# Two weight sums of a seven-product block: adding DMAs inside SBUF in place of VectorE additions

## The reference

```
h = rmsnorm(x, norm_mix);  proj = h @ w_in                    # 2048 -> 3*1024 + 4
q, k, v: 4 heads of 256;   cum = cumsum(log_sigmoid(gate logits))
p = softmax(q k^T / 16 + cum_t - cum_s, keys s <= t)
x = x + merge_heads(p v) @ w_out
h = rmsnorm(x, norm_ffn)
x = x + (silu(h @ w_gate) * (h @ w_up)) @ w_down              # 2048 -> 5632 -> 2048
out = rmsnorm(x, final_norm)
```

## Time and profile before

| What | Value |
|---|---|
| median of 3 runs | 1839.42 us (1839.38 to 1840.31) |
| the profiled execution's own time | 1841.1 us |
| its span, first to last instruction | 1839.3 us |
| mean granted TensorE clock | 0.993 |
| PE, DVE, ACT, POOL busy | 98%, 61%, 36%, 3% of the span |

### The profile page before, as it was taken

One profiled execution on the slowest core, in us unless ns is written; L12 is line 12 of the kernel. 1 busy time (PEld: TensorE's weight loads), 2 busy tenths in 40 slices (PEclk: granted clock), 3 DMA queues, 4 the chain that ended last, 5 costly groups with the idle time before them and its releaser, 6 DMA issues.

```text
span 1839.3 us, 29804 instructions
## 1 busy us (share of the span) xinstructions
PE 1807.1 (98%) x11560; PEld 1647.4 (90%) x11560; DVE 1115.5 (61%) x1277; ACT 659.0 (36%) x867; POOL 58.5 (3%) x82
## 2 busy tenths in 40 slices
PE   8999999999799999999999999999999999999998
PEld 6888888888698999989989999899899899998996
DVE  5332432337875766757757667577477575674774
ACT  5232232334342433424424324234243243342444
POOL 3000000004000000000000000000000000000005
PEclk9999999999899999999999999999999999999999
DMA  7323322332133432343333333323333333234332
GB/s 229 87 75 92 91 68 91 143 132 69 46 93 100 115 118 82 93 127 94 102 93 101 112 109 93 117 81 120 98 92 104 104 115 108 77 110 119 92 138 92
DMA packets 268389, 189.55 MB, mean 103 GB/s; under 512 B 7280, under 2 KB 236656, under 8 KB 267376
## 3 DMA queue, kind: packets, MB, share of 16 engines
q1 hardware_dynamic: 265872, 181.46, 33.7%
q10 hardware_dynamic: 2400, 6.29, 0.9%
HBM read 183.54 MB, written 4.19 MB: 102 GB/s over the span
## 4 chain that ended last, share of the span: by engine, by line
PE 92%; DVE 4%; ACT 2%; issue 1%; POOL 1%; DMA 0%; ACTq 0%; POOLq 0%; DVEq 0%
PE ps L1423 45%; PE ps L1635 31%; PE ps L1642 15%; DVE tmp L1027 1%; DVE hT_lo L1015 1%; DVE qq L1338 1%; POOL xres L656 0%; DVE sy L1338 0%; PE ps L1436 0%; DVE oT_lo L1343 0%; ACT split_hi L853 0%; DMA xres<-in_x_dram 0%; DVE split_lo L1217 0%; DVE split_lo L1008 0%; PE ps L1478 0%
## 5 line engine op out<-in xcount | busy, mean ns | idle before, releaser
L853 ACT ACTIVATE split_hi<-raw 128x1024 fp32r<-128x1024 f32 x378 | 399.9, 1058 | 781.8 <-DVE raw L1231 387.7
L1217 DVE TENSOR_TENSOR split_lo<-raw,split_hi 128x1024 fp32r<-128x1024 f32 x378 | 462.0, 1223 | 331.5 <-ACT split_hi L853 331.5
L1423 PE MATMUL ps<-split_hi,hT_hi 128*128 128x512 f32 x704 | 274.2, 389 | 1.0 <-DVE hT_lo L1259 1.0
L1423 PE MATMUL ps<-split_lo,hT_hi 128*128 128x512 f32 x704 | 274.0, 389 | 0.0
L1423 PE MATMUL ps<-split_hi,hT_lo 128*128 128x512 f32 x704 | 273.9, 389 | 0.0
L1635 PE MATMUL ps<-hT_hi,split_hi 128*128 128x256 f32 x1008 | 247.8, 284 | 0.0
L1635 PE MATMUL ps<-hT_lo,split_hi 128*128 128x256 f32 x1008 | 247.3, 283 | 0.0
L1231 DVE TENSOR_TENSOR raw<-raw 128x1024 f32<-128x1024 f32 x168 | 205.2, 1221 | 9.6
L1635 PEld LDWEIGHTS ps<-hT_hi,split_hi 128*128 128x128 f32 x1008 | 193.4, 192 | 2.2 <-issue 2.0
L1635 PEld LDWEIGHTS ps<-hT_lo,split_hi 128*128 128x128 f32 x1008 | 193.4, 192 | 0.1
L1423 PE MATMUL ps<-hT_hi,split_hi 128*128 128x512 f32 (+1 forms) x464 | 171.2, 369 | 0.8 <-DVE split_lo L1008 0.8
(11 more groups left out here) (173 smaller groups left out, 2594.3 us busy)
## 6 DMA issues: line engine op xcount, KB each, us to landing
raw<-in_ffn_w_gate_up_dram SPq DMA_DIRECT2D x172, 512.0 KB, 4.2
raw<-in_ffn_w_down_dram SPq DMA_DIRECT2D x80, 512.0 KB, 4.1
raw<-in_fox_w_in_dram SPq DMA_DIRECT2D x24, 1024.0 KB, 5.7
raw<-in_fox_w_out_dram SPq DMA_DIRECT2D x8, 1024.0 KB, 5.1
xres<-in_x_dram SPq DMA_DIRECT2D x4, 1024.0 KB, 8.2
xres<-in_x_dram ACTq DMA_DIRECT2D x4, 1024.0 KB, 8.5
raw<-in_ffn_w_down_dram SPq DMA_DIRECT2D x4, 1024.0 KB, 5.6
out_dram<-xres SPq DMA_DIRECT2D x16, 256.0 KB, 3.1
```

Source lines behind the costliest of these rows:

```text
L853: nc.scalar.activation(ring(0, n), source, ACT.Copy).then_inc(t_hi, 1)
L1217: nc.vector.tensor_tensor(ring(1, n), source, f32(ring(0, n)), ALU.subtract).then_inc(t_lo, 1)
L1423: ins = nc.tensor.matmul(bank, stationary(sp, t), moving(mp, t), start=first and t == tiles[0] and (sp, mp) == PASSES[0], stop=last and t ...
```

## The change

The third sum (B12 + B22) and the fourth (B11 + B21) are no longer made by VectorE. GpSimd issues a DMA for each, from SBUF to SBUF, which adds B22 to what lies in B12's slot, and B21 to what lies in B11's slot. `t_sum` now counts two sums per unit, and two new semaphores, `sum_in`, are raised when an adding DMA has landed; ScalarE waits for these before parts 4 and 6. Before each DMA GpSimd adds a 128 by 1 tile to itself (`turn_of`) and raises `turns`, on which the next one waits. GpSimd waits for the second sum before the first DMA, and for the low half of part 2 and B21's load before the second. SP's waits on the third and fourth sum become waits on the low halves of parts 4 and 6. ScalarE waits for the low half of part n-2 before it copies part n.

```diff
     def sums(self, j):
-        return counted(8, 16, self.r, 4 * self.nth + j)
+        return counted(4, 8, self.r, 2 * self.nth + j)
+    def summed(self):
+        return 16 * (self.nth + 1) if self.r is None else 64 * self.r + 16 * (2 + self.nth + 1)
...
# SP, load_units; the same two edits in load_group, and the second one ahead of load_last(1)
-                    sp.wait_ge(t_sum, at.sums(3))
+                    sp.wait_ge(t_lo, at.part(4))
                     load_part(r, "B22", u + 1)
...
-                    sp.wait_ge(t_sum, at.sums(4))
+                    sp.wait_ge(t_lo, at.part(6))
                     load_part(r, "B21", u + 1)
...
# GpSimd, between its work for the second norm and for the last
+            def add_part(at, j, into, other):
+                x1, x2 = (slot(place(at.r, name, at.u)[0]) for name in (into, other))
+                if at.r is not None or at.nth or j:
+                    pool.wait_ge(turns, counted(4, 8, at.r, 2 * at.nth + j))
+                nc.gpsimd.tensor_tensor(out=turn_of[:], in0=half[:], in1=half[:], op=ALU.add).then_inc(turns, 1)
+                pool.dma_start(x1, x2, accum_op=ALU.add).then_inc(sum_in[j], 16)
+            def unit_sums(at):
+                pool.wait_ge(t_sum, at.sums(2))
+                add_part(at, 0, "B12", "B22")
+                pool.wait_ge(t_lo, at.part(2))
+                wait_loaded(pool, at.r, "B21", at.u)
+                add_part(at, 1, "B11", "B21")
...
# ScalarE
                 if n >= 2:
+                    act.wait_ge(t_lo, parts(r, n - 1))
...
-                act.wait_ge(t_sum, at.sums((0, 1, 2, 0, 3, 0, 4)[e]))
+                if e < 4:
+                    act.wait_ge(t_sum, at.sums(e))
+                else:
+                    act.wait_ge(sum_in[e // 2 - 2], at.summed())
...
# VectorE, unit
                 unit_lo(at, 3)
-                dve.wait_ge(t_sum, at.sums(2))
-                sum_of(at, "B12", "B22")
...
                 unit_lo(at, 5)
-                dve.wait_ge(t_lo, at.part(2))
-                sum_of(at, "B11", "B21")
```

More of the change, by code:

```diff
@@ L217, in fox_layer @@
         half = sb("half", [P, 1])
+        turn_of = sb("turn_of", [P, 1])
         sumsq = sb("sumsq", [P, NT, NC])
@@ L357, in fox_layer @@
         t_sum = sem("t_sum")
+        sum_in = [sem(f"sum{j}_in") for j in (3, 4)]
+        turns = sem("turns")
         t_hi = sem("t_hi")
@@ L649, in _ @@
                                                 op=ALU.mult).then_inc(h_pool, 1)
+            def add_part(at, j, into, other):
[10 more added lines that the diff above has]
+                add_part(at, 1, "B11", "B21")
+            for at in units(None):
+                unit_sums(at)
+            with pool.Fori(0, GROUPS - 2) as r:
+                for at in units(r):
+                    unit_sums(at)
+            for at in units(GROUPS - 2):
+                unit_sums(at)
             pool.wait_ge(gain_in, 16 * 3)
```

## The result

| | before | changed |
|---|---|---|
| median of 5 runs | 1840.31 us | 1847.87 us (1846.88 to 1849.03) |
| ratio of the times | | 1.0041, 95% interval 1.0028 to 1.0054 |
| span of the profiled execution | 1839.3 us | 1844.8 us |

The change makes the kernel 7.6 us slower. The forecast was 23.0 us slower: the sign was right and the size three times too large. The two profiled executions lie 5.5 us apart, not 7.6: that of the changed kernel is the fastest of its five, that of the kernel before (1841.1 us) is above its median. All times compared here are of executions at a granted clock of 0.99; one of the 12 of experiment 7 ran at 0.846, took 1969 us and is left out.

The account below looks back on a forecast made before the run. TensorE was taken to bound the kernel, with 1.46 us idle in the units. Waits of 21.2 us for the first DMA plus 1.85 for the last load, 23.0, on 1839.4 gave 1862.4 us; range 1838.5 to 1945.

Parts of the forecast that it names:

- The bound, and what VectorE's relief is worth: In the 42 units TensorE bounds, with 1.46 us idle; removing 102.6 us of VectorE sums is worth 0.
- The budget of 6.12 us and what a miss costs: Second sum's end to the third sum's latest landing for part 4, in 27 units; beyond it TensorE waits.
- The first DMA's price: Third sum by DMA: 6.85 us, 0.73 over budget in 27 units, 0.37 in 4; 21.2 us of waits.
- from issue to landing: First DMA's transfer time: 5.7 us, taken from a 1024 KB load; lower end 4.2, upper 8.5.
- The tile: GpSimd's 128 x 1 addition before the first DMA: held 0.59 us by VectorE, then 0.19 us.
- ScalarE's new wait: Wait on low part n-2 before copying part n: met long before part 4's copy, so costs nothing.
- The last load: Second load of the last down projection goes out behind low part 6; its copy starts later, costing 1.85 us.
- The second DMA: Fourth sum, needed for part 6: lands at 1013.87 against 1015.24, hidden with 1.4 us to spare.
- SP's loads: B22 and B21 loads go out after low parts 4 and 6; B22 has 11 us for 4.2: nothing.
- the hidden case: Rival: first DMA lands within 5.0 us of issue, only the end costs, 1841.3 us; chance 0.29.
- the much slower case: Rival: first DMA takes 7 us or more to land, costing 78 us at 7; chance 0.27.
- The sign of the much slower case: GpSimd's small tile or DMA instruction lasting until VectorE's work ends, more than once per DMA.

Follow-up runs that it names:

- experiment 7: Changed kernel with only the fourth sum by DMA, ScalarE's added wait dropped ahead of parts 1 to 5, last load issued behind the landed sum: ratio 1.0001.
- experiment 4: Changed kernel with the first adding DMA waiting for the low half of part 2 instead of the second sum, about 2.6 us later: 1927.42 us.
- experiment 1: Kernel before, all four sums on VectorE, with only ScalarE's wait on the low half of part n-2 added: ratio 1.0029.
- second profile: Profile of the changed kernel run again, unaltered, on the same chip as the other follow-up runs: ratio 1.0054.

## Why the prediction was right and wrong

- **The bound, and what VectorE's relief is worth:** right. VectorE fell by 94.7 us and the time did not; with the costs taken away the time is that of before (experiment 7). VectorE as a whole is not off the path, though: the first and second sum are on the chain to part 2. The third and fourth, which the change removes, are not.
- **The budget of 6.12 us and what a miss costs:** right (experiment 4, 1.66 against 1.65 us).
- **The first DMA's price:** this step failed, a term of the sum that was too large. The term "from issue to landing" was 5.7 us, from a load of 1024 KB out of HBM, with 0.37 for GpSimd's issue on top. Measured, it is 4.5 to 4.9 in an ordinary unit with the issue in it. The tile was sized about right (1025.34 to 1025.90, ending 0.65 behind the second sum, where 0.78 was forecast). The sum is then 5.2 us, under the budget: 21.2 us of waits were forecast, and 2.4 to 6.0 came, by another way: not three units in four by 0.73 us each, but a few of them by 0.2 to 1.3 us. The rule of the Trainium skill's page "DMA: Bandwidth & Descriptors" (Anatomy of one DMA), set aside for the row, was nearer: for 512 KB it gives 3.2 and for twice the bytes 4.4, estimates worked out from it, against 2.9 for the copy and 4.7 for the addition. The Trainium skill's page "Collectives: The Full Stack" (The bandwidth ceiling) says of the adding step of a ring collective that it is slower because it needs two source reads. The 2.79 against 1.30 us on each engine fit that, but don't show the reads: the queue's row counts 44.05 MB for the addition and for the copy alike.
- **ScalarE's new wait:** this step failed too, the other way. It was costed at nothing since the low half is ready long before. The wait itself never holds; the operation that carries it costs 0.07 to 0.08 us each time, and the prediction named part 4's copy as the one to look at and called the copies behind it early. Part 2's copy was not early. That is 4.0 us in the profile and 5.3 by the ratio of experiment 1. The prediction's own sign of being wrong, units that are late though the DMAs land in time, is what came.
- **The sign:** right in part by luck. Slower was forecast from the DMA's waits and the last load; more than half of the loss in the first profile came from the wait that was put at nothing.
- **The last load:** mechanism right, size off: 0.66 us in place of 1.85. It lands 5.1 us after its issue (1786.06 to 1791.16), not 5.6, and low part 6, now that its copy doesn't wait for a VectorE sum, is ready 4.20 us before ScalarE's last gate copy (1786.03 against 1790.23), where it was 3.59 before.
- **The second DMA, SP's loads:** hidden, as forecast; no unit waits at part 6. The loads of 512 KB take 4.6 us to land where they took 4.2 and 4.1, within their room.
- **The rivals:** the hidden case came nearest for the DMA. It was ruled out as a whole by a cost that no rival had. The sign of the much slower case did not come: all 84 issues of GpSimd took 0.87 to 1.09 us.

## What to carry to other kernels

A wait that is always met was still not free here: in the loop it took 0.07 to 0.08 us of ScalarE's order each time. Before adding one, look for the chain that ties with the bounding engine, not only for the wait's own slack. A transfer that replaces computing has to be given room for its worst landing (6.8 us), not its median (4.5); with enough room it cost nothing here. And taking away work that the bounding engine doesn't wait for bought nothing here, so every small cost of the edit showed. One kernel was not run: both sums by DMAs, with the wait and the end mended and the first DMA given room for its worst landing.

## What the runs showed of the hardware

- An adding DMA inside SBUF, 128 x 1024 float32, issued by GpSimd: 4.7 us from issue to landing as a median of 84 (4.5 at the least, 6.4 at the most; 6.8 in the second profile), 2.9 for a copy, 3.3 for an addition of half the size.
- GpSimd's issue of it takes 0.88 us, of a copy 0.58. A 128 x 1 addition on GpSimd took 0.52 us in the mean beside VectorE's work, where a small one alone takes 0.19.
- One more wait through a register on ScalarE delayed the copy behind it by 0.07 to 0.08 us (0.19 against 0.11 behind the sum's end); outside the loop the same code left the units 20.16 us apart.
- A packet of the instruction queue holds one of the DMA engines for about 0.9 us. Where it started ahead of an adding DMA's last 4-byte packet, that DMA landed in 6.2 to 6.4 us in place of 4.5 (first profile, 4 units).
